# The second layer's output product by Strassen's scheme, on pairs of token tiles in two phases, with the sums on GpSimd

## What is computed

```python
for l in range(DEPTH):                       # 2 layers
    proj = rmsnorm(x, norm_g[l]) @ w_in[l]   # queries, gates, memory queries
    ...                                      # layer 0: recurrence; layer 1: sliding-window attention y
    om = mem_attend(...)                     # memory attention, both layers
    z = concat([y * silu(g_main), om * silu(g_mem)])   # (tokens, 1536)
    x = x + z @ w_out[l]                     # (1536, 1024): the product that is changed, for l = 1
return rmsnorm(x, final_g), ...
```

## Time and profile before

| | us |
|---|---|
| median of 3 runs | 2064.55 (2064.46 to 2065.13) |
| the profiled execution: its span | 2063.2 |
| TensorE busy | 2047.3 |
| VectorE busy | 1176.5 |
| ScalarE busy | 922.6 |
| GpSimd busy | 122.0 |

### The profile page before, as it was taken

One profiled execution on the slowest core, in us unless ns is written; L12 is line 12 of the kernel. 1 busy time (PEld: TensorE's weight loads), 2 busy tenths in 40 slices (PEclk: granted clock), 3 DMA queues, 4 the chain that ended last, 5 costly groups with the idle time before them and its releaser, 6 DMA issues.

```text
span 2063.2 us, 34681 instructions
## 1 busy us (share of the span) xinstructions
PE 2047.3 (99%) x14497; PEld 1625.4 (79%) x14497; DVE 1176.5 (57%) x2029; ACT 922.6 (45%) x2015; POOL 122.0 (6%) x138
## 2 busy tenths in 40 slices
PE   9999999999999999999999999999999999999998
PEld 7788887777777778777888888777778778777886
DVE  4845436777777842222634444688888888833232
ACT  5733335777777832222533433444444445422111
POOL 0000000000000000000200000222121220000000
PEclk9999999999999999999999999999999999999999
DMA  9311111111110565354211111122222214485352
GB/s 385 143 64 41 64 39 52 48 57 52 45 46 29 189 218 181 122 168 140 94 53 36 41 42 39 60 79 78 70 86 68 79 57 143 135 275 172 117 184 93
DMA packets 118828, 210.66 MB, mean 102 GB/s; under 512 B 12596, under 2 KB 67924, under 8 KB 114184
## 3 DMA queue, kind: packets, MB, share of 16 engines
q1 hardware_dynamic: 118672, 208.45, 29.9%
HBM read 160.00 MB, written 48.48 MB: 101 GB/s over the span
## 4 chain that ended last, share of the span: by engine, by line
PE 91%; DVE 4%; DMA 2%; ACT 1%; SPq 1%; issue 1%; DVEq 0%
PE bank L611 51%; PE bank L2094 23%; PE bank L153 2%; PE bank L715 2%; PE bank L1175 2%; PE bank L1161 2%; PE bank L702 2%; DMA in_rows<-in_x_prompt 2%; PE bank L911 1%; PE bank L451 1%; DVE wo_lo L1788 1%; PE bank L631 1%; PE bank L705 1%; DMA z_raw<-z_scratch 0%; DVE it_PTs L1249 0%
## 5 line engine op out<-in xcount | busy, mean ns | idle before, releaser
L611 PE MATMUL bank<-x_hi,w_hi 128*128 128x512 f32 x1600 | 636.1, 398 | 0.4 <-DVE w_lo L597 0.4
L611 PE MATMUL bank<-x_hi,w_lo 128*128 128x512 f32 x1600 | 624.1, 390 | 0.0
L611 PE MATMUL bank<-x_lo,w_hi 128*128 128x512 f32 x1600 | 623.1, 389 | 0.0
L611 PEld LDWEIGHTS bank<-x_hi,w_hi 128*128 128x128 f32 x1600 | 300.2, 188 | 96.7 <-issue 35.4
L611 PEld LDWEIGHTS bank<-x_hi,w_lo 128*128 128x128 f32 x1600 | 300.3, 188 | 64.5
L611 PEld LDWEIGHTS bank<-x_lo,w_hi 128*128 128x128 f32 x1600 | 300.6, 188 | 60.8 <-issue 0.7
L2094 PE MATMUL bank<-wo_hi,z_hi 128*128 128x512 f32 x768 | 303.4, 395 | 4.2 <-DVE z_lo L1817 3.7
L2094 PE MATMUL bank<-wo_lo,z_hi 128*128 128x512 f32 x768 | 299.3, 390 | 0.0
L2094 PE MATMUL bank<-wo_hi,z_lo 128*128 128x512 f32 x768 | 299.0, 389 | 0.0
L2094 PEld LDWEIGHTS bank<-wo_hi,z_hi 128*128 128x128 f32 x768 | 144.1, 188 | 43.2 <-issue 5.0
L2094 PEld LDWEIGHTS bank<-wo_hi,z_lo 128*128 128x128 f32 x768 | 144.2, 188 | 30.5
(11 more groups left out here) (324 smaller groups left out, 2624.8 us busy)
## 6 DMA issues: line engine op xcount, KB each, us to landing
w_raw<-in_w_items SPq DMA_DIRECT2D x25, 1024.0 KB, 5.1
z_scratch<-it_gz SPq DMA_DIRECT2D x96, 256.0 KB, 2.6
z_raw<-z_scratch SPq DMA_DIRECT2D x32, 768.0 KB, 5.6
it_cs<-in_rope SPq DMA_DIRECT2D x32, 512.0 KB, 4.2
wo_raw<-in_w_out SPq DMA_DIRECT2D x6, 2048.0 KB, 9.6
in_rows<-in_x_prompt SPq DMA_DIRECT2D x4, 2048.0 KB, 27.1
in_x<-in_x_T SPq DMA_DIRECT2D x4, 2048.0 KB, 28.0
z_x<-in_x_prompt SPq DMA_DIRECT2D x16, 512.0 KB, 4.1
```

The lines of the kernel that those rows point to most:

```text
L611: last = nc.tensor.matmul(ps, s_, r_, start=(k == 0 and q == 0), stop=(k == KT - 1 and q == 2))
```

## The change

`output` is no longer used for layer 1; a new function `paired` takes its place. It takes two token tiles at a time and half of the inner dimension (phase 0: blocks 0 to 5, phase 1: blocks 6 to 11), so that z's part is a matrix of 2 x 2 blocks, A11, A12, A21, A22 (128 tokens x 384), and w_out's part is B11, B12, B21, B22 (384 x 512). There are 2 phases x 8 pairs = 16 units. A unit has seven products in place of eight, P1 to P7, in the order P1, P2, P6, P5, P7, P3, P4, each of 3 x 3 = 9 matmuls: 16 x 7 x 9 = 1008 matmuls of the shape that they had.

- The sums of blocks are made by GpSimd: four for the tokens of each unit (128x384 each), and four for the weights of each phase (128x1536 each; in phase 1 the last one as three of 128x512). In phase 0 GpSimd also makes the low parts of the weights of P3 and P4 (six of 128x512).
- The seven products of a unit alternate between two of TensorE's banks and are partly added up in them; VectorE adds the bank to the residual rows after each product, seven times in a unit (128x512 each), and product i waits for the addition of product i-2.
- The residual rows are stored after phase 0 (512 KB per tile) and loaded again in phase 1, where the final norm is written over them, and the load of a unit's rows waits for the store of the unit two before.
- The loads of z are four DMAs of 192 KB for a unit in place of one of 768 KB for a tile, and wait until the unit two before is done. The weights are six loads of 768 KB in phase 0 and five in phase 1.
- VectorE's low parts of z are three instructions per unit, 128x1152, 128x768 and 128x768. In slots 32 and 33 the products of units 0 and 1 stand in `tail` (18, 18, 45 and 18 matmuls).
- The samples' steps move to units 8 to 13; some buffers move. In phase 1 SyncE issues the loads of rows and keys in unit 8, of values in unit 10, and `w_again` in units 12 and 13.

```diff
--- before
+++ after
         for q in range(NQ + 2):
             if q == 0:
                 mem_head(v, chn, G - 1)
+            ahead["first_dve"](v, q)
             if q >= 2:
                 swa_weights(v, q - 2)
+            ahead["weights_dve"](v, q)
             if 1 <= q <= NQ:
                 swa_max(v, chn, q - 1)
             if q < NQ - 1:
...
+def paired(nc, m, sem, A, outs, it, sm, prior):
...
+    P1, P2, P6, P5, P7, P3, P4 = range(NPROD)
+    A11, A12, A22, S2, S1, S3, S4 = range(7)
+    of_z = {P1: A11, P2: A12, P6: S2, P5: S1, P7: S3, P3: S4, P4: A22}
...
+    bank = lambda u, i: m.bank[2 * (u % 2) + i % 2]
+    part_of = {P1: (0, 0), P2: (0, 0), P6: (0, 512), P5: (1, 512), P7: (1, 512), P3: (0, 512), P4: (1, 0)}
+    needs = {P2: P1, P7: P5, P3: P6}
...
+    def load_z(s, u):
+        f, j, p = phase(u), u % 8, u % 2
+        it["z_stored"](s, NCH * (6 * f + 5) + j // 2)
+        if u >= 2:
+            s.wait_ge(mmd, MM0 + NPROD * (u - 1))
+        cols = lambda k, h: m.z_d[k:k + KQ, :, 256 * j + 128 * h:256 * j + 128 * h + 128].rearrange("k p t -> p k t")
+        k = 6 * f
+        s.dma_start(z_raw[p][:, A11, :, :], cols(k, 0)).then_inc(z_ld[p], 16)
+        s.dma_start(z_a21[p][:, :, :], cols(k, 1)).then_inc(z_ld[p], 16)
+        s.dma_start(z_raw[p][:, A22, :, :], cols(k + 3, 1)).then_inc(z_ld[p], 16)
+        s.dma_start(z_raw[p][:, A12, :, :], cols(k + 3, 0)).then_inc(z_ld[p], 16)
+    def load_x(s, u):
+        if u >= 2:
+            s.wait_ge(*stores(u - 2))
+        for h in range(2):
+            s.dma_start(xt[u % 2][h][:, :], rows(u, h)).then_inc(x_ld[u % 2], 16)
+    def early_sp(s, q):
+        if q == 28:
+            s.wait_ge(*after("g_done", NCH * (NW - 1)))
+            load_b(s, 0, 0, 1, b12, w_ld[0])
+            load_b(s, 0, 0, 0, b11, w_ld[0])
+        if q == 29:
+            s.wait_ge(*chunk_free(0))
+            load_b(s, 0, 0, 0, w_raw[0][P1], w_ld[1])
+        if q == 30:
+            s.wait_ge(*chunk_free(1))
+            load_b(s, 0, 1, 1, w_raw[0][P3], w_ld[2])
+            load_b(s, 0, 1, 0, w_raw[0][P2], x_ld[2])
+            load_z(s, 0)
+        if q == 31:
+            s.wait_ge(*chunk_free(2))
+            load_b(s, 0, 1, 0, w_raw[0][P4], sx[2])
+            load_x(s, 0)
...
+    def store_x(s, u):
+        for h in range(2):
+            s.wait_ge(xn, XN0 + made(u, (P3, P4)[h]))
+            s.dma_start(rows(u, h), xt[u % 2][h][:, :]).then_inc(sx[u % 2], 16)
+    def sync(s):
+        for u in range(1, UNITS):
+            if 2 <= u < UNITS - 1:
+                load_z(s, u + 1)
+            if u >= 9:
+                for h in range(2):
+                    s.wait_ge(yn, YN0 + 2 * (u - 9) + h + 1)
+                    s.dma_start(outs["y_p"][0, 256 * (u - 9) + 128 * h:256 * (u - 9) + 128 * h + 128, :], xt[(u - 1) % 2][h][:, :]).then_inc(sx[(u - 1) % 2], 16)
+            if 2 <= u < UNITS - 1:
+                load_x(s, u + 1)
+            if u == 1:
+                s.wait_ge(sums_w, SW0 + 4)
+                load_b(s, 1, 0, 0, w_raw[1][P1], w_ld[0])
+            if u == 2:
+                s.wait_ge(*after("z_ready", NI * NCH))
+                it["z_all_stored"](s)
+                load_b(s, 1, 0, 1, w_raw[1][P7], w_ld[1])
+                load_b(s, 1, 1, 1, w_raw[1][P6], w_ld[2])
+                load_b(s, 1, 1, 0, w_raw[1][P2], x_ld[2])
+            if u == 7:
+                s.wait_ge(mmd, MM0 + made(7, P3))
+                load_b(s, 1, 1, 1, w_raw[1][P3], sx[2])
+            if u < 8:
+                store_x(s, u)
+            if u == 8:
+                s.wait_ge(mmd, MM0 + NPROD * 8)
+                sm["sp"](s, 0)
+                sm["sp_keys"](s)
...
+            if u == 9:
+                sm["sp"](s, 1)
+            if u == 10:
+                sm["sp"](s, 2)
+            if u == 12:
+                s.wait_ge(sm["signals"]["pv_d"], 2)
+                for k in range(0, 8, 2):
+                    s.dma_start(w_again[:, k:k + 2, :], A["w_out"][1, k:k + 2].rearrange("k p n -> p k n")).then_inc(w_ld[0], 16)
+            if u == 13:
+                s.wait_ge(sm["zs_r"], sm["zs_0"] + 3)
+                sm["sp"](s, 6)
...
+    def sums_weights(g, f):
+        lo = w_raw[f]
+        tt = nc.gpsimd.tensor_tensor
+        if f == 0:
+            g.wait_ge(w_ld[0], WL0 + 32)
+            g.wait_ge(*chunk_free(2))
+            tt(lo[P5][:, :, :], b12[:, :, :], b11[:, :, :], ALU.subtract).then_inc(sums_w, 1)
+            g.wait_ge(w_ld[2], WL0 + 16)
+            g.wait_ge(sums_w, SW0 + 1)
+            tt(lo[P6][:, :, :], lo[P3][:, :, :], lo[P5][:, :, :], ALU.subtract).then_inc(sums_w, 1)
+            g.wait_ge(sx[2], ONE0 + 16)
+            g.wait_ge(sums_w, SW0 + 2)
+            tt(lo[P4][:, :, :], lo[P4][:, :, :], lo[P6][:, :, :], ALU.subtract).then_inc(sums_w, 1)
+            g.wait_ge(*chunk_free(3))
+            tt(lo[P7][:, :, :], lo[P3][:, :, :], b12[:, :, :], ALU.subtract).then_inc(sums_w, 1)
...
+    def sums_tokens(g, u):
+        z, n = z_raw[u % 2], SZ0 + 4 * u
+        a21 = z_a21[u % 2][:, :, :]
+        tt = nc.gpsimd.tensor_tensor
+        g.wait_ge(*z_loaded(u))
+        tt(z[:, S1, :, :], a21, z[:, A22, :, :], ALU.add).then_inc(sums_z, 1)
+        tt(z[:, S3, :, :], z[:, A11, :, :], a21, ALU.subtract).then_inc(sums_z, 1)
+        g.wait_ge(sums_z, n + 1)
+        tt(z[:, S2, :, :], z[:, S1, :, :], z[:, A11, :, :], ALU.subtract).then_inc(sums_z, 1)
+        g.wait_ge(sums_z, n + 3)
+        tt(z[:, S4, :, :], z[:, A12, :, :], z[:, S2, :, :], ALU.subtract).then_inc(sums_z, 1)
+    def pool(g):
+        sums_tokens(g, 0)
+        sums_weights(g, 0)
+        sums_tokens(g, 1)
+        for i in (P3, P4):
+            for k in range(KQ):
+                g.wait_ge(whi, W0 + KQ * i + k + 1)
+                nc.gpsimd.tensor_tensor(w_lo[0][i][:, k, :], w_raw[0][i][:, k, :], w_hi[0][i][:, k, :].bitcast(F32), ALU.subtract).then_inc(wlop, 1)
+        for u in range(2, UNITS):
+            sums_tokens(g, u)
+            if u == 3:
+                sums_weights(g, 1)
+            if u == 9:
+                sm["pool"](g)
...
+    def tokens_low(v, u, n):
+        p, e = u % 2, (slice(0, 3), slice(3, 5), slice(5, 7))[n]
+        v.wait_ge(zhi, Z0 + 2 * u + min(n, 1) + 1)
+        if n == 0:
+            v.wait_ge(sums_z, SZ0 + 4 * u + 4)
+        nc.vector.tensor_tensor(z_lo[p][:, e, :, :], z_raw[p][:, e, :, :], z_hi[p][:, e, :, :].bitcast(F32), ALU.subtract).then_inc(zlo, 1)
+    def add(v, u, i):
+        if i == 0:
+            v.wait_ge(x_ld[u % 2], LD0 + 32 * (u // 2 + 1))
+        if i in needs:
+            v.wait_ge(xn, XN0 + extra + made(u, needs[i]))
+        v.wait_ge(mmd, MM0 + (1 if u == UNITS - 1 else 0) + made(u, i))
+        x = xt[u % 2][h][:, o:o + 512]
+        nc.vector.tensor_tensor(x, x, bank(u, i), ALU.add).then_inc(xn, 1)
+    def first_dve(v, q):
+        if q == 32:
+            add(v, 0, P1)
+            weights_low(v, 0, P5)
+            add(v, 0, P2)
+        if q == 33:
+            add(v, 1, P1)
+            tokens_low(v, 1, 2)
+            add(v, 1, P2)
+    def weights_dve(v, q):
+        if q == 32:
+            add(v, 0, P6)
+            weights_low(v, 0, P7)
+            add(v, 0, P5)
+        if q == 33:
+            add(v, 1, P6)
+            add(v, 1, P5)
+    def within_dve(v, q):
+        if q == 30:
+            weights_low(v, 0, P1)
+        if q == 31:
+            for n in range(3):
+                tokens_low(v, 0, n)
+        if q == 32:
+            add(v, 0, P7)
+            tokens_low(v, 1, 0)
+    def result_dve(v, q):
+        if q == 32:
+            add(v, 0, P3)
+            add(v, 0, P4)
...
+    def vector(v, c):
+        for u in range(1, UNITS):
+            for i in range(NPROD):
+                if u > 1 or i >= P7:
+                    if u == UNITS - 1 and i == 0:
+                        add_samples(v, c)
+                    add(v, u, i)
+                if i == 0 and u > 1:
+                    tokens_low(v, u, 2)
+                if u >= 9 and i in (1, 2):
+                    norm(v, c, u - 1, i - 1)
+                if 4 <= u < 8 and 1 <= i <= 4:
+                    n = 4 * (u - 4) + i - 1
...
+    def product(pe, u, i):
+        f, p = phase(u), u % 2
+        extra = 2 if u == UNITS - 1 else 0
+        if u == 0 and i < 2:
+            pe.wait_ge(*after(("b_free", "g_free")[i], NCH * NW + 1))
+        if u == 1 and i == 0:
+            pe.wait_ge(*after("m_ready", it["G"] + it["NQ"]))
+        if i in (0, 2, 4):
+            pe.wait_ge(zlo, Z0 + 3 * u + i // 2 + 1)
+        if i >= 2:
+            pe.wait_ge(xn, XN0 + extra + made(u, i - 2))
+        a, al = (z[p][:, of_z[i], :, :] for z in (z_hi, z_lo))
+        b, bl = w_hi[f][i], w_lo[f][i]
+        for k in range(KQ):
+            if u % 8 == 0:
+                pe.wait_ge(*((wlop, WP0 + KQ * (i - P3) + k + 1) if f == 0 and i >= P3 else (wlo, W0 + low_at(f, i, k))))
```

(6 more changed lines are left out.)

314 lines of the change are left out of this document (285 added, 29 removed).

## The result

The changed kernel takes **2089.88 us** (median of 4 runs, 2086.07 to 2092.88) against 2064.81 in the 4 runs beside it (2064.46 to 2065.13). The ratio is 1.0123, 95% interval 1.0109 to 1.0137: 25.1 us slower, where 12.3 were forecast. The profiled execution spans 2091.1 us, 27.9 more than before; it is the slowest of the four (2092.88), 3 us above their median.

A forecast was written before the change was run, and what follows sets the result against it. TensorE was taken to bound the kernel, except from 1750 to 1800 us, where VectorE was nearly as busy. -32.7 + 19 + 7 + 2 + 14 + 1 + 2 = +12.3 us gave a 2075.5 us span, 2077 median; range 2052 to 2100.

The forecast's parts named there:

- 144 matmuls: Whole kernel: 1152 matmuls become 1008, at 0.227 us each, -32.7 us.
- tail: Slots 30 to 33: GpSimd's sums hold VectorE, the flip is 8.5 us late, last values at 1816.0; +19 us.
- units 3 and 4: GpSimd's phase 1 weight sums hold VectorE's low parts, and unit 4's token sums start behind them; +7 us (0 to 9).
- other units: Token load, sums and low part just fit a 14.3 us unit; 0.15 us a unit, +2 us (0 to +18).
- phase 1, samples' loads: SyncE's in-order queue delays sample sums and z in units 8, 11, 12 and 14; +14 us (5 to 20).
- end: After the last product: one more VectorE norm of 1024 columns ahead of the last rows; +1 us.
- clock behind waits: Matmuls behind long TensorE waits run at the lower clock; +2 us (0 to 8).
- alternation: VectorE and GpSimd instructions with two SBUF inputs take turns, each waiting until the other's instruction is over.
- lower bound of +4 "with no hold": Tail: the same timetable without GpSimd holding VectorE ends at 1800.8, +4 us.
- a slack of some 13 us: Phase 1 before the change: z had this slack, so none of the samples' load delays reached TensorE.
- the upper end of my 0 to 8: Clock term: up to 2 us of doubled matmuls behind each of four waits; nearer by the skill, time some 4 us higher.
- The rival that was nearest: Token load, sums and low part take 15.9 us, not 14.3; 13 units x 1.6 = 20 us more, 2097; chance 0.19.

The follow-up runs named there:

- e1: Changed kernel with GpSimd's four phase 0 weight sums cut to 16 columns and plain W_out quarters loaded in their places; 2085.51 us (1 run).
- e2: Changed kernel with GpSimd's four phase 0 weight sums (128x1536) replaced by copies of one operand; 2079.50 us (1 run).
- e4: Changed kernel with the load of final_g issued in unit 4 instead of unit 8; 2088.82 us.
- e13: Changed kernel with the samples' values and W_out's row pairs issued on ScalarE's queue, the keys staying on SyncE's; 2091.15 us.
- e5: Changed kernel with the samples' keys, values and W_out's row pairs issued in smaller lots spread over more units; 2098.65 us.
- e6: Changed kernel with the samples' keys, values and W_out's row pairs issued on ScalarE's queue in place of SyncE's; 2102.96 us.
- e11: Changed kernel with matmuls that nobody reads issued ahead of units 4, 12 and 14 and the samples' transpose in unit 8; 2091.01 us.
- e15: Changed kernel without three quarters of the samples' keys, half their values and two thirds of W_out's rows being loaded; 2075.50 us.
- e7: Changed kernel with GpSimd's phase 1 weight sums divided over units 3, 4 and 5; 2086.60 us.
- e8: Changed kernel with two of each unit's four token loads issued half a unit earlier; 2093.40 us.

## Why the prediction had the direction right and half of the size

Forecast and measured, in us of the profiled execution; the measured terms are worked out from the rows of the profile after, as the text below says:

| step | forecast | measured |
|---|---|---|
| 144 matmuls | -32.7 | -32.7 (0.227 each behind full clock, as before) |
| tail | +19 | +20.0 (last values 18.0 later, 2.0 less work) |
| units 3 and 4 | +7 | +5.9 |
| other units | +2 | +2.6 (0.37 at seven unit starts) |
| phase 1, samples' loads | +14 | +19.2 |
| end | +1 | +1.2 |
| clock behind waits | +2 | +8.5 |
| sum | +12.3 | +24.7 of 27.9 |

The 3.2 us that are left have no row. The forecast came out at half of the measured change, and two of its terms make up most of the difference, the clock (+6.5) and phase 1 (+5.2).

**The tail was right, mechanism and size.** The flip of slot 31 was forecast 8.5 us late and waits 8.01; the first product stands at 1776.40 for 1775.4; the last values end 0.9 us late of the forecast. What I had as alternation from the earlier trace rows is what the trace shows: VectorE's instructions with two SBUF inputs, from 8 to 1024 columns, wait for the end of GpSimd's. The hold of L1287 is 3.2 us (3.38 less 0.16). The Trainium skill (SBUF — State Buffer, "Who interferes with whom") says that the first to start keeps the shared ports for its whole instruction, and that GpSimd only has to read. With the sum's length from my rows that gave up to 3.5, and the trace and the run with copies agree with both. The lower bound of +4 "with no hold" was too low: with short holds (e1, e2) the tail still costs 9 us, 11 with the work that it lacks, and VectorE has next to no free time there (24.79 of 25 us busy). Some luck is in the size: the timetable had no lower clock, and by the clock's share some 5 us of TensorE's work in the tail are lost to it, counted in the 20.0.

**One step that failed is phase 1.** I put the waits at units 8, 11, 12 and 14 with 4.8, 2.9, 4.0 and 1.7; they are 3.45, 0.65, 6.18 and 6.10, and 2.54 more behind final_g, whose load stands behind the keys (11.9 us to landing, VectorE waits 4.7). That the load of W_out's rows delays unit 14 was in the list at a quarter of its size. I took the landing of one queued load from the earlier trace rows and shared it out over places. The issue of 0.38 us in the earlier trace rows was that of a load put in 3 us behind the keys; right behind the values it takes 1.8 us, over four times that. And "a slack of some 13 us" was misread. In a quiet tile of the kernel before, z's low part ends at 1874.94 and the tile that uses it starts at 1881.94, 7.0 us later:

```profile
1873.18 1.76 DVE L1817 TENSOR_TENSOR z_lo<-z_raw,z_hi 128x1536 fp32r<-128x1536 f32 x1 [0.70 <-ACT z_hi L1813]
```
```profile
1881.94 16.34 PE bank L2094 x72
```

Behind the keys it was 9.0 us (1839.57 to 1848.59), and behind the sample rows none (TensorE waited 0.24 us at 1824.13).

**The other, and the larger miss, is the clock**, 2 us put and 8.5 found: the share missing from full clock times TensorE's busy time in the stretches from 1945 to 1960, 2000 to 2010 and 2045 to 2055. By the Trainium skill (TensorE: Matmul & The Clock Gate, Part 1) the upper end of my 0 to 8 would have been nearer, and the trace agrees with 8.5, though not wait by wait: behind 3.66 us at unit 4 the clock stayed at 1.00. The filled waits show that the term is a cost of its own: with the clock up, units 12 and 14 were 5.0 us shorter. (The sum's four waits of 8.5, 3.8, 3.1 and 4.8 us also name two, 3.8 and 3.1, that no other term of it has.)

**A small one is the quiet unit**, 0.35 for 0.15. I had named the cause, the low part behind P3's addition. The slack behind it is smaller than I thought: without it, GpSimd's last sum is next after 0.3 us.

**The rival that was nearest** was the token chain longer than a unit, 2097 from +20. Its total is nearer to the result than mine (2097 and 2077 for 2090), but that is luck, for its picture is not what the trace shows: not 1.6 us in every unit, but 0.35 in the quiet ones and 6 in two that have the samples' loads.

**What the parts cost.** Making the sums copies gives back 24.5 us, taking two thirds of the samples' large loads out 14.4, together more than the 25.1 that the change lost. That is no contradiction: the change lost 25.1 net of 32.7 us of matmuls saved, so 57.8 us of new cost stand against the saving. Of what the copies give back, by the profiles, 14.0 us are in the loop (VectorE held beside GpSimd), 6 in units 3 and 4 (the weight sums) and 4 at units 12 and 14. Only these last lie in one chain with the loads: token load, four sums, low part, first product. A unit of 14.3 us has no slack for both, the earlier tile of 16.36 us had 7. The change took 2 us off each tile's matmuls, the work that had covered this chain, and put 4 us of sums into it.

**What stays open** is why runs of one of these kernels differ by 3 to 12 us, those of before by 1 to 4. The profiles show three places where kernels with the same instructions part: VectorE's low part for unit 3 starts just ahead of GpSimd's first weight sum (changed, e4, e13: no wait) or 0.1 to 0.9 us behind its start (e1, e5, e6, e11, e15: TensorE waits 2.5 to 3.3 us at unit 3), VectorE waits for final_g 1.9 us (e7, e13, where unit 9 takes 23 us) or 4.7 (changed and e8, 28 and 27 us), and the clock behind the same wait of 3.66 us at unit 4 stays up or falls (14.65 us in the changed kernel, 17.12 in e4). Why they come out as they do is not tested.

## What to carry to other kernels

Price a saving of matmuls against what those matmuls covered: write down the chain of the next tile (load, sums, rounding, low part) at its length with the queue as full as it will be, and compare it with the shorter tile; here 32.7 us of matmuls bought a slack that was needed. Weigh what a repair gives back against the whole new cost, not against the net loss. Work given to GpSimd isn't free while VectorE is full: in these runs each of GpSimd's sums and copies in SBUF held a VectorE instruction with two SBUF inputs for up to the whole of its own length. When one repair after another moves a wait and gains nothing, take out a whole resource (all sums, most bytes) to see which one the time hangs on. And read a small difference against kernels that have the same instructions in that stretch.

## What the runs showed of the hardware

- GpSimd's copy of 128x1536 takes 1.5 to 1.7 us, its subtraction 3.4 to 4.2 in the tail. Both hold VectorE's instruction with two SBUF inputs to their end, down to one of 8 columns.
- With keys, values and W_out's rows on ScalarE's queue, the loads of SyncE's queue shared with them: the token loads landed sooner (waits of 15.9 us became 3.5), two window loads of 512 KB later, after 12.5 and 16.0 us in place of 3.7 and 4.5.
- An issue of a token load takes 0.4 to 0.9 us in SyncE's queue in quiet units, and 1.5 to 1.9 behind the eight loads of values of 512 KB.
- The clock fell from 2.4 to 1.2 GHz behind waits of 2.54, 6.18 and 6.10 us (0.50 in the worst 5 us). Behind one of 3.66 us it stayed up in the changed kernel (1.00 from 1860 to 1865) and fell in e4 (0.58 and 0.73). Matmuls that nobody reads kept it at 1.00 at units 12 and 14 (e11), and these units were 5.0 us shorter.
